# A longer run of full-precision blocks, six dots ahead of the first pair, and a new rule for raw slots, in a two-layer conv / MLA / PEER trunk

## The reference, cut to what matters

```python
def peer(x, w_q, sub_keys, u, v):
    ...
    experts = (i1 * PEER_N_KEYS + i2).reshape(T, PEER_HEADS * PEER_TOPK)     # 128 of 16384 a token
    gates = jax.nn.softmax(cv, axis=-1).reshape(T, PEER_HEADS * PEER_TOPK)
    ...
        ub = jnp.take(u, eb, axis=0)
        a = jax.nn.gelu(jnp.einsum('td,tkd->tk', xb, ub), approximate=False) * gb
        vb = jnp.take(v, eb, axis=0)
        return jnp.einsum('tk,tkd->td', a, vb)
```

## Time and profile before

| | |
|---|---|
| three runs | 1611.72 us median, 1608.25 to 1613.63 |
| the profiled execution, its own time | 1608.02 us |
| its span, first to last instruction | 1606.2 us |
| busy PE / DVE / ACT / POOL | 97% / 84% / 39% / 38% |
| granted TensorE clock, mean | 0.994 |
| HBM read | 488.79 MB, 305 GB/s over the span |

### The profile page before, as it was taken

The page is one execution under the profiler, slowest core; times in us unless marked ns, Lnnn a source line. Parts: engine busy times, 40 slices in busy tenths (PEclk is TensorE's granted clock), DMA queues, the critical chain, the costliest instruction groups (busy, mean ns, idle before and its releaser), DMA issues. The chain is left out here.

```text
span 1606.2 us, 27972 instructions
## 1 busy us (share of the span) xinstructions
PE 1558.4 (97%) x10766; PEld 1499.4 (93%) x10766; DVE 1343.0 (84%) x2549; ACT 625.2 (39%) x1145; POOL 603.7 (38%) x438
## 2 busy tenths in 40 slices
PE   9999999999999999999899999998999999999988
PEld 9978999989999999999788899998999999999986
DVE  7986696999998998888666749959999988888875
ACT  5563221333334444544535441123333344444442
POOL 6741003745443554552004200156444435555410
PEclk9999999999999999999999999999999999999999
DMA  7644579999999999999633237799999999999980
GB/s 256 217 148 156 174 220 328 366 393 387 374 364 372 390 406 403 402 404 374 259 113 119 80 123 258 231 374 366 389 374 376 366 365 407 408 406 408 406 314 27
DMA packets 136965, 493.95 MB, mean 308 GB/s; under 512 B 16064, under 2 KB 16576, under 8 KB 136576
## 3 DMA queue, kind: packets, MB, share of 16 engines
q1 hardware_dynamic: 85248, 307.42, 51.8%
q0 software_dynamic: 47552, 170.06, 27.7%
q10 hardware_dynamic: 4032, 14.68, 2.6%
HBM read 488.79 MB, written 1.05 MB: 305 GB/s over the span
## 5 line engine op out<-in xcount | busy, mean ns | idle before, releaser
L678 POOL DMA_INDIRECT big<-v,picks x160 | 255.3, 1596 | 263.2 <-DVE big L1916 207.6
L678 POOL DMA_INDIRECT big<-u_rows,picks x160 | 221.1, 1382 | 229.9 <-DVE big L1832 200.5
L716 PE MATMUL work<-columns,raw 128*128 128x176 f32 x1920 | 298.9, 314 | 1.1 <-DVE big L1810 0.8
L716 PEld LDWEIGHTS work<-columns,raw 128*128 128x128 f32 x1920 | 288.2, 190 | 2.2 <-issue 1.9
L612 DVE TENSOR_TENSOR low<-raw,high 128x1024 fp32r<-128x1024 f32 x181 | 226.7, 1255 | 40.7 <-ACT high L1237 40.5
L1237 ACT ACTIVATE high<-raw 128x1024 fp32r<-128x1024 f32 x197 | 205.9, 1048 | 35.8 <-PE work L781 11.4
L1916 DVE SCALAR_TENSOR_TENSOR big<-big,side_hid 128x1024 f32<-128x1024 f32 x156 | 199.7, 1280 | 2.3
L1832 DVE SCALAR_TENSOR_TENSOR big<-big 128x1024 f32<-128x1024 f32 x160 | 190.0, 1220 | 6.7 <-DMA big<-u_rows,picks 6.7
L1498 ACT ACTIVATE xT<-big 128x176 fp32r<-128x176 f32 x198 | 67.5, 349 | 248.3 <-PE work L861 194.3
L716 PE MATMUL work<-columns,extra_raw 128*128 128x176 f32 x896 | 142.6, 315 | 4.7 <-DVE big L1810 4.6
L856 PE MATMUL y<-xT,high 128*128 128x352 f32 x600 | 133.9, 345 | 9.1 <-DVE xT L1887 9.1
(11 more groups left out here) (262 smaller groups left out, 2859.7 us busy)
## 6 DMA issues: line engine op xcount, KB each, us to landing
raw<-u SPq DMA_DIRECT2D x172, 512.0 KB, 6.5
raw<-v SPq DMA_DIRECT2D x172, 512.0 KB, 7.8
extra_raw<-u SPq DMA_DIRECT2D x84, 512.0 KB, 6.1
extra_raw<-v SPq DMA_DIRECT2D x84, 512.0 KB, 8.4
raw<-wq SPq DMA_DIRECT2D x32, 512.0 KB, 3.8
raw<-conv_in SPq DMA_DIRECT2D x14, 512.0 KB, 4.6
aux<-ln_par ACTq DMA_DIRECT2D x9, 512.0 KB, 9.2
raw<-conv_out SPq DMA_DIRECT2D x8, 512.0 KB, 3.8
```

What stands on the lines that cost most here:

```text
L678: nc.gpsimd.indirect_dma_start(out=side_rows[n % SIDE_BUFS], out_offset=None, in_=rows, in_offset=bass.IndirectOffsetOnAxis(ap=pick_ids[:, ...
L716: mm = nc.tensor.matmul(out_, raw_at(c)[:, k * P:(k + 1) * P], x_full[:, k, :], start=(k == 0), stop=(k == KD - 1))
```

## The change

Three edits. FULL_PAIRS, which was pairs 1, 3, 5 and the 22 even pairs up to 42, becomes those 22 and pairs 1, 5, 9, ..., 41: 33 of 45 pairs are full, 12 are merged (3, 7, ..., 39, and 43 and 44) where 20 were. The dots of a layer, which came two a pair in pairs 1 to 6 and then 68 over pairs 7 to 43, become six ahead of the first pair, and 74 over pairs 0 to 42. And the planner gives a block the slot that is free first by an estimate, `released`: a full block's slot just after the block, a split one's at the block during which its high half is made by `last_high`.

```diff
-FULL_PAIRS = {1, 3, 5, *PAIR_OF}
+FULL_PAIRS = {*PAIR_OF, *range(1, PAIRS - 3, 4)}
...
-FIRST_DOTS = 12
+FIRST_DOTS = SIDE_BUFS
...
-    _at = 1 + _d // 2 if _d < FIRST_DOTS else 7 + (_d - FIRST_DOTS) * (PAIRS - 8) // (SIDE_ROWS - FIRST_DOTS)
+    _at = -1 if _d < FIRST_DOTS else (_d - FIRST_DOTS) * (PAIRS - 2) // (SIDE_ROWS - FIRST_DOTS)
...
+def released(c):
+
+    if c in FULL:
+        return c + 1
+    return min((b for b in range(max(0, c - 2 * KD), c) if last_high(b) >= c), default=c) if c >= FIRST["u0"] else c
...
-    _slot = min(range(RAW + len(extra_rooms(_c))), key=lambda slot: _last.get(slot, slot - 2 * RAW))
+    _slot = min(range(RAW + len(extra_rooms(_c))), key=lambda slot: _free.get(slot, slot - 2 * RAW))
...
-    _last[_slot] = _c
+    _last[_slot], _free[_slot] = _c, released(_c)
...
                 low_stage(u0 + EARLY + 2, u0 + EARLY + 4)
+                for d in DOT_PAIRS[-1]:
+                    side_dot(layer, d)
                 for pair in range(PAIRS):
```

More of the change, by code:

```diff
@@ L218, in extra_rooms, with last_high @@
     return ()
+def last_high(c):
+    n = c - FIRST["v0"] if c < FIRST["mla_in"] else c - FIRST["v1"]
+    return min(_g - 1, c + RING + max(0, n - GROW_FROM + 1) // GROW_EVERY)
+def released(c):
+    if c in FULL:
+        return c + 1
+    return min((b for b in range(max(0, c - 2 * KD), c) if last_high(b) >= c), default=c) if c >= FIRST["u0"] else c
 RAW_SLOT, BEFORE, LANDED, HIGHS, LOWS = {}, {}, {}, {}, {}
-_last, _loads, _lows, _highs = {}, {}, {}, 0
+_last, _free, _loads, _lows, _highs = {}, {}, {}, {}, 0
 for _c in range(_g):
-    _slot = min(range(RAW + len(extra_rooms(_c))), key=lambda slot: _last.get(slot, slot - 2 * RAW))
+    _slot = min(range(RAW + len(extra_rooms(_c))), key=lambda slot: _free.get(slot, slot - 2 * RAW))
     if _slot in _last:
         BEFORE[_c] = _last[_slot]
-    _last[_slot] = _c
+    _last[_slot], _free[_slot] = _c, released(_c)
     _loads[_slot] = _loads.get(_slot, 0) + 1
@@ L234 @@
 SLOTS = 1 + max(RAW_SLOT.values())
-def last_high(c):
-    n = c - FIRST["v0"] if c < FIRST["mla_in"] else c - FIRST["v1"]
-    return min(_g - 1, c + RING + max(0, n - GROW_FROM + 1) // GROW_EVERY)
 def a_after(c):
```

## The result

The changed kernel takes 1625.09 us (median of seven runs, 1621.42 to 1626.14), where the kernel before takes 1611.72 beside it. The ratio is 1.0072, with a 95% interval of 1.0051 to 1.0094. It is slower by 0.7%; 1598.5 was forecast, and the range ended at 1612. The profiled run took 1625.09 us and its span is 1623.2.

The account below looks back on a forecast made before the run. PE was taken to set the time, stalled by DVE, late by throughput. Layer 0 at -5.6 and layer 1 at -7.6 us gave -13.2, from a median of 1611.7 to 1598.5, range 1584 to 1612.

Parts of the forecast that it names:

- stalls gone, more PE work: Late u stages: eight more full pairs a layer remove stalls of 14.9 and 16.9 us, adding 2.8 us PE work each.
- front: Six dots before pair 0 wait for gathers: PE stalls 6.5 us at pair 2, plus 2 half clock, 8.5 a layer.
- slot rule in u, with DVE's margins: Late u stage: loads behind merged pairs just in time and DVE's order with zero margins, together 3.5 us a layer.
- end of v: Last v blocks: earlier slots remove most of the 4 us wait, smaller waits and half clock, 5.5 us a layer.
- r: Stall allowance in the late u stage for slot rule and DVE's zero margins: 3.5 us a layer, between 0 and 6.
- Rival (a): End of v: transfers set the pace, so 1 us is won instead of 5.5; -4, 1608; chance 0.17.
- T+8.6: In u, T ends PE's pair 4k; 8.6 us later DVE ends the first low half of merged pair 4k+3.
- Rival (b): In u, the first load behind each merged pair comes 1.5 us late, twenty times: +10, 1622; chance 0.10.
- DVE near 87%: Sign in the u stage: DVE's busy share falls from 97% to about 87%, so its throughput no longer limits.
- waits for the late product under 8 us a layer outside the front: Sign in the late u pairs: PE's waits for DVE's product stay under 8 us a layer, front excluded.
- the wait at pair 2 with the lower clock behind it: Sign at pair 2 of each layer: one PE wait of 6 to 7 us, then the clock at the lower level.
- PE waiting for raw loads: Sign in u that the forecast is wrong: PE waits for raw loads, because loads behind merged pairs come late.

Follow-up runs that it names:

- the best kernel: Kernel before with 33 full pairs, slot rule in v alone, 80 dots spread evenly over pairs 1 to 42, none in front: 1582.87 us, ratio 0.9821.
- the later estimate: Changed kernel with dots where they were before and a merged u block's slot counted free at the block itself: 1585.25 us, ratio 0.9839.

## Why the prediction was wrong

By its own sum, in the changed kernel (layer 0 and 1 together), and the price of each edit taken apart:

| term | forecast | changed kernel | by itself |
|---|---|---|---|
| stalls gone, more PE work | -26.2 | -26.0 | -14.2 (pairs alone, stages; with stalls that stayed) |
| front | +17.0 | +20.6 | +18.3, +17.9 |
| slot rule in u, with DVE's margins | +7.0 | +27.2 | +29.6, +31.6 (rule, old dots), about 0 (margins) |
| end of v | -11.0 | -7.1 | -10.5 |
| sum | -13.2 | +14.7 | |

How the third column is made: the stalls of before, 14.8 + 16.8, are counted as gone, against 5.6 us of PE work; what the stages now hold over PE's work, 26.0 + 21.8, is new, 20.6 of it at the front and 27.2 elsewhere; the v pieces are measured. The fourth column takes differences of medians (of stages in its first row).

**What bounds the kernel** was read rightly: PE, kept waiting by a DVE at 97%. With 33 full pairs and the slots in turn DVE is 87% busy (173.9 of 200), as foreseen, and PE 199.75 of 200.

**More full pairs** had the right sign, the right mechanism and the right PE work: stages of 232.2 to 236.6 us in the kernels with 33 full pairs, slots in turn in u and the rule in v, but no six dots in front, against 228.5 of work (the forecast's 233.3 with pair 0 taken off). The pairs alone left 11.7 us of stalls in the two stages. I had put what stays into r with the positions of the dots as changed, so those 11.7 can't be held against it: with the dots as changed and the slots in turn no wait over 0.3 us stood outside the front.

**The front**: 8.5 a layer forecast, 9.0 and 9.1 measured by itself, 10.9 and 9.7 in the changed kernel. Both bounds (3 and 12) hold it. The mechanism was right in each step: SP held by a low half, gathers with 79.3% of the queues' time, DVE behind dot 5. What I had too low, in the changed kernel, was PE's wait at pair 2 (6.5 forecast, 8.7 and 7.6 measured); in layer 0 the gathers started later against pair 0: in the execution of before they were issued 4.1 us ahead of the first late block, here 2.4.

**The end of v**: 5.5 a layer forecast, 5.2 by itself. In the changed kernel it was 3.6, partly because a wait of 1.9 us in layer 0 was again followed by PE at the lower clock. Rival (a), transfers as the limit, is out: v ran at 406 GB/s for 200 us, and the best kernel had 396 in u. The 358 GB/s per core of the Trainium skill (DMA: Bandwidth & Descriptors, Specifications) did not bind in any run here.

**The step that failed is the slot rule in u.** The prediction named the wait (SP, in order, for the low half of the pair's first block at T+8.6, "the loads behind it wait too"), and then priced only the first of these loads: it finds its queue empty and lands in 5 to 7 us, just in time. That load is in time; its median was 4.9 us. The price falls on the loads behind it. SP stands up to 12 us and then issues six loads in 5.3 us, the last four in 1.7; the next merged pair's own first block joins behind them and lands in 12.0 us (median 10.1) where 6 to 7 is usual. ACT, DVE's low half, two dots and the product follow in order, and PE is up to 2.7 us late in the changed kernel, up to 3.7 in the one with the old dots. So the term of 3.5 us a layer became 15.1 and 12.1. As that low half is late, SP is also let go late again, so the delay may feed itself from pair to pair; this is argued from one turn, and the waits don't grow steadily (in layer 0 they are 1.4, 2.6, 0.2, 0.5, none, none, 0.2, 1.3 and 1.2 us ahead of pairs 7 to 39). The prediction also priced one held load behind each merged pair, where there are two. Rival (b) had the sign and, at 1622, nearly the time, but its mechanism (the first load late by 1.5 us, twenty times) is not what happened, and its nearness is luck; it got 0.10, since I asked of each load alone whether it would be in time.

What was expected to show: DVE near 87% (82.9; 87.0 without the rule), waits for the late product under 8 us a layer outside the front (11.1 in layer 0: not so; 7.7 in layer 1), the wait at pair 2 with the lower clock behind it (so), the end of v near 1 us (1.9 and 1.3). The sign named for (b), PE waiting for raw loads, would not have shown the fault: PE's waits name DVE, and the late load stands behind its low half and product.

**Open**: why the rule is harmless with 20 merged pairs (its slots differ, as told above), whether a rule that leaves strict turns in u can be harmless with 33 full pairs, why front and rule together cost some 10 us less than apart (1585.25 + 17.9 + 31.6 = 1634.7, and 1625.1 was measured; while PE waits in front, late loads catch up, perhaps), and the last two waits of the best kernel.

## What to carry to other kernels

When an in-order queue is made to wait, price the whole burst behind the wait, not the first transfer: ask which later block joins that burst, and whether its lateness delays the very event that the queue waits for. A rule that picks the buffer "free first" trusts an estimate of when a buffer comes free, and one that is too early makes the whole queue wait: here it cost about 30 us in u. Before testing a variant of such a rule, print what it chooses: here the later estimate chose the strict turns again, and the same rule chose other slots with other pairs. Work moved to an idle engine's gap needs its data there too: two dots in front cost 1.5 us or nothing, six cost 9 us a layer.

## What the runs showed of the hardware

With the old dots, two raw loads of 512 KB that SP issued after a wait of 11.7 us landed after 4.4 us (median), and one behind a burst of four after 12.0. With the slots in turn, most loads 2.4 us apart, the median was 7.2: the same transfer, by what stood ahead of it.

PE's clock did not follow the length of a wait alone. After 2.56 us of idle time, at 334.60, the granted clock was 1.00 and eight records took 1.52 us; after 2.65 us, at 513.03, the second eight took 1.85 us instead of 1.02 (granted clock 0.57 from 514 to 518); and after 1.88 us at the end of v two chunks took 1.52 us each, where 0.83 is usual (0.54 from 787.7 to 791.0):

```profile
513.03 1.62 PE L743 MATMUL work<-xT,high 128*128 128x352 f32 x8 [2.65 <-DVE big L1817]
514.45 1.85 PE L746 MATMUL work<-xT,low 128*128 128x176 f32 x8
...
786.69 0.72 PE L863 MATMUL y<-xT,high 128*128 128x352 f32 x3 [1.88 <-DVE xT L1896]
...
787.71 1.15 PE L863 MATMUL y<-xT,high 128*128 128x352 f32 x3
...
789.23 1.15 PE L863 MATMUL y<-xT,high 128*128 128x352 f32 x3
```

What decides it the runs don't tell. On top of the wait a fall to the lower level (1.2 of 2.4 GHz) cost 2.2 and 2.1 us at pair 2, and 1.6 us in each of the two places above.
